# A hybrid encoder step on one NeuronCore: the projection's loop over seven groups of rows, written out on all engines

## What is computed

```python
proj = h @ w_in                      # 1024 -> 3080
x_lru, y_lru, qkv, z, b_logit, a_logit = ...columns of proj...
xc, new_conv_l = causal_conv(x_lru, conv_l, lru_cw); xc = xc + lru_cb
r, i = sigmoid(xc @ wa + ba), sigmoid(xc @ wx + bx)      # in blocks of 64
a = exp(-8 * r * softplus(-lam)); b = sqrt(1 - a * a) * (i * xc)
h_t = a_t * h_{t-1} + b_t            # a scan over the rows
out_a = h * gelu(y_lru)
qkv_c = silu(causal_conv(qkv, conv_g, gdn_cw)); z = silu(z)
```

## Time and profile before

| | |
|---|---|
| median of 3 runs | 4064.1 us (4056.6 to 4073.2) |
| the profiled execution | 4061.4 us, its span 4059.8 us |
| busy over the span | PE 3477.0 us (86%), DVE 1831.0 (45%), ACT 1321.8 (33%), POOL 862.3 (21%) |
| code moved over the span | queue q8 91 packets, 1.49 MB; queue q14 85 packets, 0.70 MB |

### The profile page before, as it was taken

The page is one execution under the profiler, slowest core; times in us unless marked ns, Lnnn a source line. Parts: engine busy times, 40 slices in busy tenths (PEclk is TensorE's granted clock), DMA queues, the critical chain, the costliest instruction groups (busy, mean ns, idle before and its releaser), DMA issues. The chain is left out here.

```text
span 4059.8 us, 60667 instructions
## 1 busy us (share of the span) xinstructions
PE 3477.0 (86%) x17482; PEld 2084.2 (51%) x17483; DVE 1831.0 (45%) x4821; ACT 1321.8 (33%) x2601; POOL 862.3 (21%) x1018
## 2 busy tenths in 40 slices
PE   7999999999985488889889888849999999999920
PEld 3444444444455477767767766624444444444410
DVE  6565455456443356666666666531111111111158
ACT  7455455545552133333333333301111111111122
POOL 0000000000001143444444444311111111111157
PEclk9999999999996599999899999979999999999965
DMA  4311111111112344344343443235455556553268
GB/s 144 108 47 49 49 52 49 49 67 39 36 37 91 87 145 129 108 135 126 105 140 106 125 118 109 81 122 202 177 197 220 202 191 227 225 198 116 91 251 312
DMA packets 335728, 514.03 MB, mean 127 GB/s; under 512 B 79968, under 2 KB 228928, under 8 KB 327104
## 3 DMA queue, kind: packets, MB, share of 16 engines
q1 hardware_dynamic: 252400, 279.19, 21.7%
q10 hardware_dynamic: 54288, 146.56, 9.2%
q0 software_dynamic: 28864, 86.09, 6.5%
HBM read 341.49 MB, written 170.26 MB: 126 GB/s over the span
## 5 line engine op out<-in xcount | busy, mean ns | idle before, releaser
L1757 PE MATMUL ebank<-w,rowsT 128*128 x1568 | 703.5, 602 | 32.6 <-SPq L1698 29.3
L300 PE MATMUL pP<-h_hi,w_hi 128*128 128x512 f16 (+1 forms) x1728 | 625.8, 366 | 31.5 <-DVE h_lo L482 16.8
L300 PE MATMUL pP<-h_lo,w_hi 128*128 128x512 f16 (+1 forms) x1728 | 625.4, 366 | 0.0
L300 PE MATMUL pP<-h_hi,w_lo 128*128 128x512 f16 (+1 forms) x1728 | 625.0, 366 | 0.0
L1757 PEld LDWEIGHTS ebank<-w,rowsT 128*128 128x128 f32 x1568 | 301.1, 193 | 420.8 <-issue 420.8
L1775 PE MATMUL ebank<-w,guT 128*128 x784 | 353.4, 593 | 2.6 <-ACT guT L1796 2.6
L1824 DVE TENSOR_TENSOR gu<-ebank,sil 128x256 f32<-128x256 f32 x98 | 41.6, 425 | 696.1 <-ACT sil L1792 696.1
L513 DVE SCALAR_TENSOR_TENSOR cv<-win,cols_sb,cv 128x512 f32<-128x512 f32 (+1 forms) x432 | 305.4, 707 | 35.1 <-issue 3.6
L1792 ACT ACTIVATE sil<-ebank 128x256 f32<-128x256 f32 x98 | 37.7, 384 | 818.2 <-PE ebank L1757 818.2
L300 PEld LDWEIGHTS pP<-h_hi,w_hi 128*128 128x128 f16 x1728 | 172.2, 100 | 221.3 <-issue 31.7
L300 PEld LDWEIGHTS pP<-h_lo,w_hi 128*128 128x128 f16 x1728 | 172.3, 100 | 187.8 <-issue 14.0
(11 more groups left out here) (314 smaller groups left out, 6267.3 us busy)
## 6 DMA issues: line engine op xcount, KB each, us to landing
w<-in_w SPq DMA_DIRECT2D x32, 2048.0 KB, 8.9
y<-yb ACTq DMA_DIRECT2D x98, 512.0 KB, 4.9
ft<-mixin SPq DMA_DIRECT2D x33, 1280.0 KB, 8.6
mixin<-qo ACTq DMA_DIRECT2D x128, 256.0 KB, 2.0
w<-in_w SPq DMA_DIRECT2D x32, 1024.0 KB, 12.1
xt<-in_x SPq DMA_DIRECT2D x33, 512.0 KB, 5.1
kz<-mixin SPq DMA_DIRECT2D x33, 512.0 KB, 4.5
xr<-in_x SPq DMA_DIRECT2D x33, 512.0 KB, 5.5
```

The source lines that it names most:

```text
L300: ins = nc.tensor.matmul(pP[n % NPB][:, 0:N], w[:, k, c0:c0 + P], h[:, k, 0:N], start=(k + i == 0), stop=(k == KD - 1 and i == 2))
L1757: ins = nc.tensor.matmul((M0, M1)[p][:, :], xT[p][:, k, :], w13[:, bass.ds(s, 1), k * 512:(k + 1) * 512].rearrange("p a n -> p (a n)"), st ...
```

## The change

Five loops of the program become Python loops, so the kernel holds each group's instructions once for each group, with the group's number a constant. Nothing else is changed: the same groups, the same steps in the same order, the same waits with constants in the place of registers.

```diff
--- before.py
+++ after.py
@@ -227,7 +227,7 @@
                 if n >= 2:
                     sp.wait_ge(w_split, n - 1)
                 sp.dma_start(stage[:, n % 2, :, 0:w], T["w_in"][:, :, c:c + w]).then_inc(weights_in[n % 2], 16)
-            with sp.Fori(2, groups) as g:
+            for g in range(2, groups):
                 load(g, GT)
             load(groups, 1)
 
@@ -262,7 +262,7 @@
                 pool.wait_ge(*xs_did.at("xs", g, back=1))
                 nc.gpsimd.tensor_tensor(rs[:, 0:n], ss[:, 0:n], neghalf[:, 0:n], ALU.pow).then_inc(*rs_did.did("rs"))
 
-            with pool.Fori(0, groups) as g:
+            for g in range(0, groups):
                 group(g, GT)
             group(groups, 1)
 
@@ -322,7 +322,7 @@
                         ins.then_inc(*pe_did.did("B0"))
 
             group(0, GT, first=True)
-            with pe.Fori(1, groups) as g:
+            for g in range(1, groups):
                 group(g, GT)
             group(groups, 1)
 
@@ -447,7 +447,7 @@
             split(0)
             split(1)
             group(0, GT, False, GT, first=True)
-            with act.Fori(1, groups - 1) as g:
+            for g in range(1, groups - 1):
                 group(g, GT, False, GT)
             group(groups - 1, GT, False, 1)
             group(groups, 1, True, 0)
@@ -564,7 +564,7 @@
             split(0)
             split(1)
             group(0, GT, False, GT, first=True)
-            with dve.Fori(1, groups - 1) as g:
+            for g in range(1, groups - 1):
                 group(g, GT, False, GT)
             group(groups - 1, GT, False, 1)
             group(groups, 1, True, 0)
```

## The result

The changed kernel took 4070.2 us (median of 11 runs, 4059.0 to 4078.1), the kernel before 4052.1 on the same chip (11 runs): ratio 1.0043, 95% interval 1.0025 to 1.0062. It is slower, by 18 us. Forecast were 4060 us, 0.89 for no change and 0.05 for slower. The time lies inside the range given, and 0.43% inside the 0.5% that the forecast took for the least that can be told; but eleven runs of each tell it, and the direction isn't the forecast one.

The account below looks back on a forecast made before the run. TensorE was taken to bound the projection, with 4.8 us of idle a pass. Savings of 3.05 + 0.5 + 1.6 - 0.8 = 4.4 us took 4061.4 to 4057.0 us, forecast as 4060 for the median; range 4046 to 4072.

Parts of the forecast that it names:

- Start of a group: Projection, first transpose to first h_hi: shrinks to 1.25 us in straight code, saving 3.05 us over groups 1 to 7.
- registers between the waits: Projection, TensorE from last h_lo to first matmul: 0.07 us less in each of seven groups, 0.5 us saved.
- gates: Projection, second pair of gate matmuls: ScalarE's and VectorE's register work goes, 1.6 us saved over groups 1 to 6.
- The code: Projection: fetching the written-out code costs 0 to 1.6 us over seven groups; 0.8 us taken as loss.
- its turns had cost no stop: Rival, projection: TensorE's six loop turns each held a 3.4 to 4.0 us stop, giving about 4038 us; chance 0.03.
- the granted clock: Projection, group 2: busy 140.09 us at PEclk 0.99 put down to a clock below full level, not to any instruction.
- I take 0: Mixing stage: TensorE's four loop turns could gain or lose 15 us by where the code stands; 0 taken.
- the starved TensorE: Rival, projection: straight code arrives too late, 3.4 us at some 36 packets, 122 us slower, 4182 us; chance 0.05.

Follow-up runs that it names:

- b_pe_only: Kernel before with only TensorE's projection loop written out; ratio 1.0059 to the kernel before.
- b_sp_code: Kernel before with idle instructions added on SyncE, 3700 ahead of its loop and 4800 behind its last load; ratio 1.0392.
- b_gap: Kernel before with one unused 0.6 MB input declared ahead of the others, 16 KB of it read; ratio 1.0027.
- a_gap06: Changed kernel with an unused 0.6 MB input declared ahead of the others; ratio 1.0052 to the kernel before.
- a_gap18: Changed kernel with an unused 1.8 MB input declared ahead of the others; ratio 0.9981 to the kernel before.
- b_gap25: Kernel before with an unused 2.47 MB input declared ahead of the others; ratio 1.0065.
- b_act_shift75: Kernel before with 75 idle instructions added on ScalarE behind its last projection step, shifting its later code; ratio 1.0003.
- b_code: Kernel before with 2400 idle instructions on TensorE and 2400 on SyncE added in the last stage; ratio 1.0048.

## Why the prediction was wrong

*The projection's terms* held in two of three. Start of a group, registers between the waits, and gates were forecast at 3.05 + 0.5 + 1.6 = 5.15 us; without the stretches at the low clock the seven passes went from 1005.2 - 2 x 1.7 = 1001.8 to 7 x 142.42 = 996.9 us, 4.9 us less. The 0.5 us for TensorE's registers is nothing: b_pe_only has the matmul 0.07 us earlier and the pass of 143.22 us where it was 143.23, because the next wait, for the tanh, hangs on ScalarE and takes the 0.07 back. The prediction had added up idle places as if each stood alone. With ScalarE and VectorE alone straight the pass is 142.42 us, the same as in the changed kernel.

*The code* was put at 0.8 us for the projection, and no row shows a cost: start and gates were to give 4.65 us, and 4.9 came. TensorE was never starved, and its turns had cost no stop (143.23 us with them, 143.22 without).

*The first failing step: the granted clock was taken as given.* Of group 2's low clock the prediction said that it is "the granted clock" and "no instruction", and left it out of the sum. It follows the wait for the last h_lo, and the passes that have it went from two to five: 3 x 1.7 = 5.1 us, which ate the 4.9. It varies from run to run, but over all profiles without fillers (b_sp_code aside) the passes of 143.2 us had it 10 times in 49 (0 to 2 of seven in a profile), those of 142.4 us 24 times in 49 (3 to 5 of seven). That is two passes more, 3.4 us, on average. The five kernels with fillers show the link with the idle: in their 35 passes it never comes.

*The second, which made the sign: everything outside the loops was taken to stay.* Of the stages behind the projection only the mixing stage's code got a term, "I take 0". Nothing speaks against it: ScalarE's new stops cost nothing that the ratios tell. That the two profiles differ by only 0.6 us there is luck, since the stage moves by 15 us between profiles of one kernel. The experts' stage had no term and no rival, and gave 11.1 us in the first pair of profiles and 17.0 in the second. The failing step is this silent zero: a stage whose instructions don't change was taken to keep its time. The runs showed instead that its weight loads land later (12.5 and 12.7 us, 12.1 and 12.2 before), and that an unused input does the same, or undoes it, with no instruction in play but the one small load (b_gap, a_gap06, a_gap18). The reading of this is that the 0.68 MB of instructions are also bytes in the device's memory, and that the data then lie elsewhere.

Of the rivals the starved TensorE, which would have been slower too, was refuted. Nothing in the rows named what did happen; but the waits for the experts' weights, 29.3 us in 15 places on the path, were in the profile and would have carried a range: 3% on a landing of 12.1 us is 11 us of time.

*What stays open.* The trace shows no addresses. That the loads depend on where data lie in memory is the reading of the gap experiments, of which a_gap06 and a_gap18 differ in nothing but the gap's size; whether it is the weights, the other arrays or the instructions whose place counts isn't shown, and no kernel with a gap was profiled twice (those without one repeat their landing to 0.2 us). Which address is a good one isn't shown, and the sum of bytes (b_gap25) doesn't give it. Why the clock falls behind one idle place and not behind the same one in the next group, and why it does so more often in the shorter pass, isn't shown either. b_act_shift75 had a landing of 12.2 us and still 1174.9 us in the experts' stage, with nine stretches at the low clock: there, too, one profile of a kernel is good to some 7 us. And the written-out loops as such are worth nothing that can be told beside the 0.6 to 0.7% by which the places differ: over three places each the ratios are 1.0000, 1.0027, 1.0065 for the instructions of before, and 1.0043, 1.0052, 0.9981 for the changed ones.

## What to carry to other kernels

A change in the amount of code or in the inputs can make loads that are waited for far away faster or slower, by more than the change is worth: here 0.65% from an input of which 16 KB are read. Compare stage by stage the landing time of loads that nothing touched before you explain a difference under 1%, and judge such a change over several placements (an unused input of another size each). Before you count register work saved on one engine, ask which engine the next wait hangs on: TensorE's 0.07 us a pass was gone by the next wait. Where idle of 1 to 2 us stands between dense stretches of matmuls, shortening it may not pay as long as any is left; filling it with matmuls that do nothing did: the projection ended at 1233 to 1235 us instead of 1240 to 1244.

## What the hardware showed that was not expected

- The same 2 MB + 1 MB loads in the same kind of stage took 12.1 to 12.9 us from issue to landing, by nothing but an unused input or other instructions, while the packets of a 2 MB load took 5.8 us per DMA engine in both kernels and 6.0 in b_gap25.
- 0.8 us of longer landing went with 21 to 25 us over 32 experts (before against b_gap25 and b_code): TensorE waits for them at 15 places only, but with longer waits come more stretches at 1.2 GHz, 1.7 us a piece (1 in a_gap18, 6 before, 14 in a_gap06).
- Twelve extra matmuls a group made the program shorter: 2.4 us of work in idle places, 1.7 us back for each pass that no longer had a stretch at the low clock, and a mixing stage that was shorter too.
- The mixing stage of one and the same kernel took 1471.6 and 1485.7 us in two executions, with 384 and 422 us at the low clock.
- ScalarE's mixing loop stayed loaded or was fetched anew (0.2 or 4.4 to 7.1 us a turn) by where it stood in the code (75 idle instructions ahead of it, and queue q14 carried 0.87 MB instead of 0.70), without an effect on the time that could be told.
